# A bidirectional state-space scan: joining the two directions' exponents by a predicated copy instead of mask products

## The chip, the cores and the metric

One core of one Trainium2 chip. The time is device microseconds of one launch; lower is better. All data are fp32, or fp32r, a rounded form in which a product shows as one record instead of two.

## What is computed

Two blocks on 256 tokens of width 1024: the first joins a bidirectional state-space branch (SSD) and windowed attention and is followed by a feed-forward layer, the second has neighbourhood attention, a short convolution and another feed-forward layer. The change is in the state-space branch alone. Cut to what matters:

```python
def segsum_exp(a):
    cs = jnp.cumsum(a, axis=-1)
    diff = cs[..., :, None] - cs[..., None, :]
    mask = jnp.tril(jnp.ones((L, L), dtype=bool))
    return jnp.exp(jnp.where(mask, diff, -jnp.inf))

def ssd_scan(x, dt, a, b, c):          # 8 groups of 4 heads of 64, state 128, chunks of 128
    a_cs = jnp.cumsum(a_dt, axis=-1)
    xdt = x * dt[..., None]
    decay = segsum_exp(a_dt)
    cb = jnp.einsum('bclgn,bcsgn->bcgls', c, b)
    y_diag = jnp.einsum('bcgls,bcgrls,bcsgrp->bclgrp', cb, decay, xdt)
    ...
    y_off = jnp.einsum('bclgn,bcgrpn,bcgrl->bclgrp', c, prev, jnp.exp(a_cs))
    return (y_diag + y_off).reshape(Bsz, S, G, R, P)

y_fwd = ssd_scan(xs, dt[:, :, 0], a[0], bs, cs)
y_bwd = fl(ssd_scan(fl(xs), fl(dt[:, :, 1]), a[1], fl(bs), fl(cs)))
y = y_fwd + y_bwd + xs * d_skip
```

The forward direction fills the triangle s <= l of the decay matrix, the backward one the triangle s >= l. They share only the diagonal, where both exponents of the decay are 0.

## The kernel before, in words

Each engine has its own hand-written program. The weights come as 147 pieces of 128x2048, one per *slot*. For a slot ScalarE makes the rounded high part (`split_hi`, L1068), VectorE the rest (`split_lo`, L1452), both two slots ahead, and TensorE multiplies (`stream`, L606). In a slot of the z and gate projections that is twelve 128x512 products, then what `slot_middle` (L897) puts between, then twelve more. Semaphores order everything: `claim` (L374) makes TensorE wait until the last reader of a PSUM bank is done, `fill_of` and `drain_of` count fills and reads, `ready` and `emptied` wait for them.

The scan runs beside slots 27 to 36, one group g per slot, g = slot - 28. In the order of TensorE, for group g and chunks c of 128 tokens:

- at the end of slot g + 27: `ssd_cb(g)` (L881, bank 7), two fp32 products of 128x128, and `ssd_decay(g, 0)` (L856, banks 5 and 6);
- in the middle of slot g + 28: `ssd_decay(g, 1)`, again into banks 5 and 6, then `ssd_states(g-1)` (bank 7), `ssd_diagonal(g-1)` (L835, bank 4) and `ssd_across(g-1)` (bank 7).

`ssd_decay` makes, for each direction d, four heads' exponents in one product of `cum_s` and `cum_l`. The tables already hold the cumulative sums and the logarithm of dt. Onto this it adds a second product, of the identity `unit` and the mask tile `far`, which holds -1e30 outside the triangle, so that the exponential is 0 there:

```python
pe.matmul(ps[:, 5 + d, :], cum_s[g % 2][:, 2 * c + d, :], cum_l[c][:, d, :, :],
          start=True, stop=False)
pe.matmul(ps[:, 5 + d, :], unit[:, :], far[:, d].unsqueeze(1).to_broadcast([P, PER_GROUP, P]),
          start=False, stop=True).then_inc(*fill_of(key))
```

ScalarE's slot (from L1218) copies `cb` out of bank 7, does `decay_exps(g, 0)` (L1149: one exponential per direction, into `decay` and `decay_back`), then `split_hi(s + 2)`, later the squares of group g - 2, `decay_exps(g, 1)`, the state copy, and after the slots in which a z chunk closes (28 and 30) a Silu of z. VectorE's slot starts with `ssd_weigh(g, 0)` (L1702: add the two directions, multiply by cb), then `split_lo(s + 2)`, `ssd_weigh(g, 1)` and `ssd_gate(g - 1)` (L1713: skip term, y_off from bank 7, y from bank 4, z), and in two of these slots a gate bias. GpSimd makes the state inputs and the rows of the cumulative sums that a group needs, `decay_rows` (L2074). ScalarE's Exp and Silu lie in different function tables, so a table load stands where they alternate.

## Time and profile before

| | |
|---|---|
| median of 3 runs | 943.63 us (942.15 to 943.77) |
| the profiled execution | 942.23 us, of which the span of the instructions is 940.4 us |
| busy in the span | TensorE 932.4 us, VectorE 662.4, ScalarE 507.6, GpSimd 60.8 |
| the scan | about 203 to 298 us |

A busy TensorE row counts a product from its start to its end, and these overlap: what a product costs is the distance from its start to the next start. In a timeline row, "x4" means that four instructions in a row are merged, and the brackets at its end give how long the engine stood idle before it and what released it.

### The profile page before, as it was taken

What the parts mean: (1) busy time and instruction counts of PE and PEld (TensorE: products, weight loads), DVE (VectorE), ACT (ScalarE), POOL (GpSimd) and SP (SyncE); (2) the same over time, 40 slices, a digit from 0 to 9 for tenths busy, and PEclk for the clock granted to TensorE, in tenths of its full rate; (3) what the DMA queues carried; (4) which work ended last, traced back from release to release, by engine and by line L of the source; (5) the groups of instructions that cost most, each with busy time, mean ns of one, the idle gap of its engine ahead of it and who ended that gap; (6) DMA issues with size and microseconds to landing.
All of it is one profiled execution on the core that took longest, in us unless ns stands there. A gap on an engine that the chain in (4) does not pass through costs nothing.

```text
span 940.4 us, 13246 instructions
## 1 busy us (share of the span) xinstructions
PE 932.4 (99%) x5362; PEld 807.9 (86%) x5362; DVE 662.4 (70%) x946; ACT 507.6 (54%) x664; POOL 60.8 (6%) x68
## 2 busy tenths in 40 slices
PE   9999999999999999999999999999999999999998
PEld 8988899988888888888888888899888898888887
DVE  6779789998878764778776446767665758776433
ACT  6457876676555733456554335755653455554331
POOL 1000000023321000000003310000000000000000
PEclk9999999999999999999999999999999999999999
DMA  8943233554224475435447955353355435546551
GB/s 306 341 168 124 93 133 135 180 167 169 91 90 157 140 307 197 169 131 221 179 180 236 256 196 206 136 205 128 123 217 179 179 135 217 187 179 224 178 179 45
DMA packets 25278, 166.51 MB, mean 177 GB/s; under 512 B 2987, under 2 KB 3115, under 8 KB 6657
## 3 DMA queue, kind: packets, MB, share of 16 engines
q1 hardware_dynamic: 22464, 156.12, 46.1%
q0 software_dynamic: 2752, 9.54, 3.5%
q8 instruction: 43, 0.70, 0.3%
q14 instruction: 19, 0.15, 0.0%
HBM read 164.57 MB, written 1.08 MB: 176 GB/s over the span
## 4 chain that ended last, share of the span: by engine, by line
PE 86%; DVE 11%; ACT 2%; issue 1%; ACTq 0%; DVEq 0%
PE ps L393 54%; PE ps L582 11%; PE ps L587 6%; DVE conv_acc L1688 5%; DVE w_lo L1455 3%; PE ps L843 1%; PE ps L772 1%; PE ps L787 1%; PE ps L424 1%; PE ps L426 1%; PE ps L433 1%; PE ps L512 1%; PE ps L630 1%; PE ps L893 1%; PE ps L852 1%
## 5 line engine op out<-in xcount | busy, mean ns | idle before, releaser
L1455 DVE TENSOR_TENSOR w_lo<-raw,w_hi 128x2048 fp32r<-128x2048 f32 x145 | 331.3, 2291 | 181.0 <-ACT w_hi L1075 180.8
L1075 ACT ACTIVATE w_hi<-raw 128x2048 fp32r<-128x2048 f32 x145 | 275.5, 1906 | 179.1 <-PE ps L393 160.2
L393 PE MATMUL ps<-w_hi,ht 128*128 128x512 f32 (+1 forms) x576 | 181.4, 388 | 0.0
L393 PE MATMUL ps<-ht,w_hi 128*128 128x256 f32 (+1 forms) x816 | 150.6, 286 | 0.0
L393 PEld LDWEIGHTS ps<-ht,w_hi 128*128 128x128 f32 (+1 forms) x816 | 126.2, 190 | 4.1 <-issue 4.0
L393 PEld LDWEIGHTS ps<-w_hi,ht 128*128 128x128 f32 x576 | 107.3, 188 | 22.4 <-issue 1.1
L393 PE MATMUL ps<-ht,w_lo 128*128 128x256 f32 (+1 forms) x408 | 115.3, 282 | 0.0
L393 PE MATMUL ps<-w_lo,ht 128*128 128x512 f32 (+1 forms) x288 | 110.5, 384 | 0.0
L582 PE MATMUL ps<-ht,w_hi 128*128 128x512 f32 x448 | 109.5, 391 | 0.0
L393 PE MATMUL ps<-w_hi,ff_hi 128*128 128x512 f32 x256 | 99.7, 389 | 0.0
L393 PE MATMUL ps<-w_lo,ff_hi 128*128 128x512 f32 x256 | 99.6, 389 | 0.0
L393 PE MATMUL ps<-w_hi,ff_lo 128*128 128x512 f32 x256 | 99.6, 389 | 0.0
L582 PEld LDWEIGHTS ps<-ht,w_hi 128*128 128x128 f32 x448 | 81.5, 189 | 15.2
L393 PEld LDWEIGHTS ps<-ht,w_lo 128*128 128x128 f32 (+1 forms) x408 | 77.6, 190 | 0.0
L393 PEld LDWEIGHTS ps<-w_lo,ht 128*128 128x128 f32 x288 | 54.2, 188 | 10.4
L587 PEld LDWEIGHTS ps<-ht,w_lo 128*128 128x128 f32 x448 | 59.3, 191 | 3.3
L587 PE MATMUL ps<-ht,w_lo 128*128 128x256 f32 x448 | 60.3, 282 | 0.0
L393 PEld LDWEIGHTS ps<-w_hi,ff_hi 128*128 128x128 f32 x256 | 48.1, 188 | 10.0
L393 PEld LDWEIGHTS ps<-w_hi,ff_lo 128*128 128x128 f32 x256 | 48.0, 188 | 10.0
L393 PEld LDWEIGHTS ps<-w_lo,ff_hi 128*128 128x128 f32 x256 | 48.1, 188 | 9.8
L1688 DVE SCALAR_TENSOR_TENSOR conv_acc<-conv_in,params,conv_acc 128x256 f32<-128x256 f32 x128 | 52.1, 477 | 0.0
L1190 ACT ACTIVATE ff_sum<-ps 128x512 f32<-128x512 f32 x32 | 18.8, 595 | 35.4 <-PE ps L587 34.4
(301 smaller groups left out, 1217.4 us busy)
## 6 DMA issues: line engine op xcount, KB each, us to landing
raw<-in_w_stream SPq DMA_DIRECT2D x145, 1024.0 KB, 4.8
bias<-rel_scratch POOLq DMA_DIRECT2D x1, 3072.0 KB, 21.2
bias<-in_rpb POOLq DMA_DIRECT2D x16, 128.0 KB, 7.9
x_first<-in_x_in SPq DMA_DIRECT2D x2, 512.0 KB, 4.1
raw<-in_w_stream SPq DMA_DIRECT2D x2, 512.0 KB, 6.4
gates<-in_gate_bias POOLq DMA_DIRECT2D x4, 256.0 KB, 6.0
gates<-in_gate_bias POOLq DMA_DIRECT2D x2, 512.0 KB, 7.2
x<-in_x_in POOLq DMA_DIRECT2D x1, 1024.0 KB, 5.3
```

The lines of the kernel that those rows point to most:

```text
L393: ins = pe.matmul(o, still, moving, start=first and n == 0, stop=last and n == 2, skip_group_check=True)
L424: pe.matmul(ps[:, i, 0:TOK], hi[:, c], ht_hi[:, k, :], start=opens and kt == 0, stop=False, skip_group_check=True)
L426: pe.matmul(ps[:, i, 0:TOK], lo[:, c], ht_hi[:, k, :], start=False, stop=False, skip_group_check=True)
L433: ins = pe.matmul(ps[:, i, TOK:2 * TOK], hi[:, kt * 512 + i * P:kt * 512 + i * P + P], ht_lo[:, 4 * part + kt, :], start=False, stop=close ...
L512: pe.matmul(ps[:, bank0 + r, :], ht_hi[:, 4 * part + kt, tokens], w[:, kt * 512:kt * 512 + 512], start=part == 0 and kt == 0 and m == 0, s ...
L582: pe.matmul(ps[:, 4 * (chunk % 2) + i, :], hi[:, cols(kt, i)], ht[:, :, 4 * part + kt, :], start=opens and kt == 0, stop=False, skip_group ...
L587: ins = pe.matmul(ps[:, 4 * (chunk % 2) + i, 0:TOK], lo[:, cols(kt, i)], ht_hi[:, 4 * part + kt, :], start=False, stop=closes and kt == 3, ...
L630: pe.matmul(ps[:, 2 * n + r, :], a_hi[:, kt, r * P:r * P + P], w[:, cols], start=kt == 0 and m == 0, stop=False, skip_group_check=True)
L1075: act.activation(split_home(s)[0][:, 0:width(s)], raw[s % RAW_RING][:, 0:width(s)], ACT.Copy).then_inc(hi_ready, 1)
L1190: act.activation(ff_sum[half][:, :, :], ps[:, b:b + 2, TOK:2 * TOK], ACT.Copy).then_inc(lows_out, 1)
L1455: dve.tensor_tensor(lo[:, 0:width(s)], raw[s % RAW_RING][:, 0:width(s)], hi[:, 0:width(s)].bitcast(F32), ALU.subtract).then_inc(lo_ready, 1)
L1688: ins = dve.scalar_tensor_tensor(acc_of(c)[:, i, :], conv_in[k][:, i, tap:tap + TOK], conv_w[:, tap, f:f + 1], acc_of(c)[:, i, :], ALU.mul ...
```

## The change

The mask products go. Both directions' exponents still land in banks 5 and 6. VectorE then copies, where s > l, bank 6 over bank 5 (`copy_predicated`, in PSUM, with the 0/1 triangle `tri[:, 2]` as predicate), and ScalarE takes one exponential of bank 5 per chunk. The addition of the two directions goes. On the diagonal only the forward value is left, so the backward direction's own term is computed apart: `twins` = B times C, summed over the state by 16 products with a column of ones, times dt, added to the skip factor once (`own_terms`). The rows of the cumulative sums of groups 1 to 7 move from GpSimd to ScalarE, behind its exponentials. ScalarE's first exponential of a slot moves behind its weight split, its second behind the state copy. VectorE's second weighing moves into the gate of the group before, behind the skip term.

```diff
+        twins = at("twins", [P, GROUPS, TOK], 146496)
+        own_skip = at("own_skip", [P, RT, HEADS], 158784)
...
                 pe.wait_ge(cum_s_ready, g + 1)
-                if g == 0 and c == 0:
-                    pe.wait_ge(far_ready, 1)
                 for d in range(2):
                     key = ("decay", g, c, d)
                     claim(key, 5 + d)
                     pe.matmul(ps[:, 5 + d, :], cum_s[g % 2][:, 2 * c + d, :], cum_l[c][:, d, :, :],
-                              start=True, stop=False)
-                    pe.matmul(ps[:, 5 + d, :], unit[:, :], far[:, d].unsqueeze(1).to_broadcast([P, PER_GROUP, P]),
-                              start=False, stop=True).then_inc(*fill_of(key))
+                              start=True, stop=True).then_inc(*fill_of(key))
+
+            def twin_sums():
+
+                claim("twins", 4)
+                pe.wait_ge(twins_ready, 1)
+                for c in range(RT):
+                    for g in range(GROUPS):
+                        at0 = c * GROUPS + g
+                        ins = pe.matmul(ps[:, 4, at0:at0 + 1], twins[:, g, c * P:c * P + P], tri[:, 0, P - 1:P],
+                                        start=True, stop=True)
+                ins.then_inc(*fill_of("twins"))
...
                     ssd_decay(s - 28, 1)
+                    if s == 28:
+                        twin_sums()
...
             def decay_exps(g, c):
-                for d, dest in enumerate((decay[g % 2][c], decay_back[c])):
-                    key = ("decay", g, c, d)
-                    ready(act, key)
-                    if d == 0 and g >= 2:
-                        ready(act, ("y", g - 2))
-                    if d == 1 and g:
-                        act.wait_ge(decay_scaled, 2 * g - 1 + c)
-                    act.activation(dest[:, :, :], ps[:, 5 + d, :].rearrange("p (h l) -> p h l", h=PER_GROUP),
-                                   ACT.Exp).then_inc(*drain_of(key))
+                key = ("decay", g, c, 0)
+                emptied(act, ("decay", g, c, 1))
+                if g == 1 and c == 0:
+                    ready(act, "twins")
+                if g >= 2:
+                    ready(act, ("y", g - 2))
+                act.activation(decay[g % 2][c][:, :, :], ps[:, 5, :].rearrange("p (h l) -> p h l", h=PER_GROUP),
+                               ACT.Exp).then_inc(*drain_of(key))
...
                                    ACT.Copy).then_inc(*drain_of(key))
-                    decay_exps(g, 0)
                 late = s in (S_MI - 1, S_MI2 - 1)
                 if s + AHEAD < SLOTS and s != S_Q2 - 1 and not late:
                     split_hi(s + AHEAD)
                 if s == S_Q2 - 2:
                     split_hi(S_Q2 + 1)
+                if 0 <= s - 28 < GROUPS:
+                    decay_exps(s - 28, 0)
...
-                if 0 <= s - 28 < GROUPS:
-                    decay_exps(s - 28, 1)
                 if 0 <= s - 29 < GROUPS:
                     key = ("state", s - 29)
                     ready(act, key)
                     act.activation(state[:, :, :], ps[:, 7, :].rearrange("p (a b) -> p a b", a=2),
                                    ACT.Copy).then_inc(*drain_of(key))
+                if 0 <= s - 28 < GROUPS:
+                    decay_exps(s - 28, 1)
+                if 0 <= s - 28 < GROUPS - 1:
+                    g = s - 27
+                    if g == 1:
+                        act.wait_ge(cum_s_ready, 1)
+                    else:
+                        ready(act, ("decay", g - 2, 1, 1))
+                    act.activation(cum_s[g % 2][:, :, :], cum[:, :, :], ACT.Identity, scale=quad[:, 10 + g:11 + g],
+                                   bias=quad[:, 18 + g:19 + g]).then_inc(cum_s_ready, 1)
...
+            def ssd_choose(g, c):
+
+                ready(dve, ("decay", g, c, 0)), ready(dve, ("decay", g, c, 1))
+                both = [ps[:, 5 + d, :].rearrange("p (h l) -> p h l", h=PER_GROUP) for d in range(2)]
+                dve.copy_predicated(both[0], tri[:, 2].bitcast(I32).unsqueeze(1).to_broadcast([P, PER_GROUP, P]),
+                                    both[1]).then_inc(*drain_of(("decay", g, c, 1)))
+
             def ssd_weigh(g, c):
 
-                emptied(dve, ("decay", g, c, 0)), emptied(dve, ("decay", g, c, 1))
-                w = decay[g % 2][c]
-                link(dve.tensor_tensor(w[:, :, :], w[:, :, :], decay_back[c][:, :, :], ALU.add))
+                emptied(dve, ("decay", g, c, 0))
...
+            def own_terms():
+
+                ready(dve, "twins")
...
                 for c in range(RT):
                     v = xtok(c, g * GW, GW).rearrange("p (h d) -> p h d", h=PER_GROUP)
-                    ins = dve.tensor_tensor(v, v, per_head(param("d_skip")[:, 4 * g:4 * g + 4], 4), ALU.mult)
+                    ins = dve.tensor_tensor(v, v, per_head(own_skip[:, c, 4 * g:4 * g + 4], 4), ALU.mult)
                 link(ins)
+                if g + 1 < GROUPS:
+                    ssd_weigh(g + 1, 1)
...
                 if 0 <= s - 28 < GROUPS:
-                    ssd_weigh(s - 28, 0)
+                    ssd_choose(s - 28, 0)
...
+                if s == 27:
+                    dve.wait_ge(conv_silu, 8)
+                    dve.tensor_tensor(twins[:, :, :], bc[:, 0:GROUPS, :], bc[:, GROUPS:2 * GROUPS, :],
+                                      ALU.mult).then_inc(twins_ready, 1)
                 if 0 <= s - 28 < GROUPS:
-                    ssd_weigh(s - 28, 1)
+                    ssd_weigh(s - 28, 0)
+                    ssd_choose(s - 28, 1)
+                if s == 28:
+                    ssd_weigh(0, 1)
+                    own_terms()
```

How the instructions now stand, at three places. First ScalarE, in the slots of groups 0 and 1; `w_hi` is the high part of a weight piece. Before:

```order
L1075 ACTIVATE w_hi_54<-raw_51 128x2048
L1227 ACTIVATE cb<-ps 128x256
L1157 ACT_TABLE_LOAD
L1157 ACTIVATE decay_0_107<-ps 128x512
L1157 ACTIVATE decay_back_111<-ps 128x512
L1075 ACTIVATE w_hi_52<-raw_49 128x2048
L1157 ACTIVATE decay_1_108<-ps 128x512
L1157 ACTIVATE decay_back_112<-ps 128x512
L1329 ACT_TABLE_LOAD
L1329 ACTIVATE zg_90<-ps 128x512 x2
L1227 ACTIVATE cb<-ps 128x256
L1157 ACT_TABLE_LOAD
```

With the change:

```order
L1083 ACTIVATE w_hi_54<-raw_51 128x2048
L1234 ACTIVATE cb<-ps 128x256
L1083 ACTIVATE w_hi_52<-raw_49 128x2048
L1164 ACT_TABLE_LOAD
L1164 ACTIVATE decay_0_107<-ps 128x512
L1164 ACTIVATE decay_1_108<-ps 128x512
L1339 ACTIVATE cum_s_124<-cum,params 128x512
L1345 ACT_TABLE_LOAD
L1345 ACTIVATE zg_90<-ps 128x512 x2
L1234 ACTIVATE cb<-ps 128x256
L1083 ACTIVATE w_hi_53<-raw_50 128x2048
L1164 ACT_TABLE_LOAD
```

The first exponential of each slot, with its table load, now stands behind the weight split, and there is one exponential per chunk.

Second VectorE, from the subtraction for slot 28 to the first work of group 1; `w_lo` is the low part of a weight piece. Before:

```order
L1455 TENSOR_TENSOR w_lo_56<-raw_50,w_hi_53 128x2048
L1455 TENSOR_TENSOR w_lo_57<-raw_51,w_hi_54 128x2048
L1706 TENSOR_TENSOR decay_0_107<-decay_0_107,decay_back_111 128x512
L1709 TENSOR_TENSOR decay_0_107<-decay_0_107,cb 128x512
L1455 TENSOR_TENSOR w_lo_55<-raw_49,w_hi_52 128x2048
L1706 TENSOR_TENSOR decay_1_108<-decay_1_108,decay_back_112 128x512
L1709 TENSOR_TENSOR decay_1_108<-decay_1_108,cb 128x512
L1706 TENSOR_TENSOR decay_0_109<-decay_0_109,decay_back_111 128x512
L1709 TENSOR_TENSOR decay_0_109<-decay_0_109,cb 128x512
```

With the change:

```order
L1471 TENSOR_TENSOR w_lo_56<-raw_50,w_hi_53 128x2048
L1471 TENSOR_TENSOR w_lo_57<-raw_51,w_hi_54 128x2048
L1925 TENSOR_TENSOR twins<-bc 128x2048
L1722 COPY_PREDICATED ps<-params,ps 128x512
L1471 TENSOR_TENSOR w_lo_55<-raw_49,w_hi_52 128x2048
L1731 TENSOR_TENSOR decay_0_107<-decay_0_107,cb 128x512
L1722 COPY_PREDICATED ps<-params,ps 128x512
L1731 TENSOR_TENSOR decay_1_108<-decay_1_108,cb 128x512
L1740 TENSOR_TENSOR own_skip<-dt,ps 128x32 x2
L1745 TENSOR_TENSOR own_skip<-own_skip,params 128x64
```

The product of B and C stands ahead of the first predicated copy, and the copies stand where the weighing of the same chunk stood.

Third TensorE, in the middle of the slot of group 0, with the change; before, four products (two of them of `far`) stood between the stream products, and no `twins`:

```order
L392 MATMUL ps<-w_hi_53,ht 128x512 x2
L392 MATMUL ps<-w_lo_56,ht 128x512
L392 MATMUL ps<-w_hi_53,ht 128x512
L862 MATMUL ps<-cum_l_122,cum_s_123 128x512 x2
L872 MATMUL ps<-params,twins 128x1 x16
L392 MATMUL ps<-w_hi_53,ht 128x512
L392 MATMUL ps<-w_lo_56,ht 128x512
```

The 16 one-column products come behind the second chunk's exponents of group 0, once in the program.

## Rows read from the trace of the kernel before

**Rows 1.** The page: busy time by engine, the clock by slice, the chain that ended last.
```profile
PE 932.4 (99%) x5362; PEld 807.9 (86%) x5362; DVE 662.4 (70%) x946; ACT 507.6 (54%) x664; POOL 60.8 (6%) x68
...
PEclk9999999999999999999999999999999999999999
...
PE 86%; DVE 11%; ACT 2%; issue 1%; ACTq 0%; DVEq 0%
```

**Rows 2.** List of waits, TensorE: us in total, times, longest.
```profile
PE ps L915 <- DVE warm L1474: 1.5, 1, 1.5
```

**Rows 3.** Timeline, TensorE, groups 3 and 4: start us, duration us, instruction.
```profile
246.33 0.48 PE L865 MATMUL ps<-cum_l,cum_s 128*128 128x512 f32 x1
...
257.32 0.60 PE L884 MATMUL ps<-bc 128*128 128x128 f32 x4
257.68 0.48 PE L865 MATMUL ps<-cum_l,cum_s 128*128 128x512 f32 x1
```

**Rows 4.** Timeline, TensorE, middle of the slot of group 1.
```profile
215.27 0.39 PE L865 MATMUL ps<-cum_l,cum_s 128*128 128x512 f32 x1
...
216.19 1.02 PE L852 MATMUL ps<-x_state,btok 128*128 128x256 f32 x4
```

**Rows 5.** Timeline, TensorE: products of 32 and of 64 moving columns, and what follows.
```profile
68.03 0.98 PE L831 MATMUL ps<-adt,params 128*128 128x32 f32 x8
68.84 0.63 PE L787 MATMUL ps<-params,logit 128*128 128x128 f32 x4
...
217.05 1.89 PE L843 MATMUL ps<-xtok,decay 128*128 128x64 f32 x16
218.78 1.08 PE L893 MATMUL ps<-state,bc 128*128 128x256 f32 x4
```

**Rows 6.** Timeline, TensorE, slot of group 0.
```profile
203.69 0.48 PE L865 MATMUL ps<-cum_l,cum_s 128*128 128x512 f32 x1
204.01 0.40 PE L867 MATMUL ps<-far,unit 128*128 128x512 f32 x1
...
207.47 0.40 PE L865 MATMUL ps<-cum_l,cum_s 128*128 128x512 f32 x1
```

**Rows 7.** Timeline, ScalarE, slot of group 4.
```profile
257.96 0.39 ACT L1227 ACTIVATE cb<-ps 128x256 f32<-128x256 f32 x1 [5.26 <-PE ps L884]
...
259.40 1.92 ACT L1075 ACTIVATE w_hi<-raw 128x2048 fp32r<-128x2048 f32 x1
261.20 0.41 ACT L1316 ACTIVATE junk<-xtok 128x256 f32<-128x256 f32 x1
```

**Rows 8.** Timeline, ScalarE, slot of group 0.
```profile
204.61 1.28 ACT L1157 ACT_TABLE_LOAD   x1
205.90 0.60 ACT L1157 ACTIVATE decay<-ps 128x512 f32<-128x512 f32 x1
```

**Rows 9.** Timeline, VectorE, slots of groups 0 and 1: weight subtractions and what follows.
```profile
204.36 2.46 DVE L1455 TENSOR_TENSOR w_lo<-raw,w_hi 128x2048 fp32r<-128x2048 f32 x1 [0.73 <-ACT w_hi L1075]
...
217.16 2.29 DVE L1455 TENSOR_TENSOR w_lo<-raw,w_hi 128x2048 fp32r<-128x2048 f32 x1 [0.31 <-ACT w_hi L1075]
219.37 1.10 DVE L1706 TENSOR_TENSOR decay<-decay,decay_back 128x512 f32<-128x512 f32 x1
```

**Rows 10.** Timeline, TensorE: first exponents of groups 1, 2 and 3.
```profile
211.52 0.48 PE L865 MATMUL ps<-cum_l,cum_s 128*128 128x512 f32 x1
...
223.48 0.48 PE L865 MATMUL ps<-cum_l,cum_s 128*128 128x512 f32 x1
...
234.82 0.48 PE L865 MATMUL ps<-cum_l,cum_s 128*128 128x512 f32 x1
```

**Rows 11.** One line's instructions, VectorE: duration ns min/median/max, first and last start.
```profile
L1728 DVE TENSOR_TENSOR xtok<-ps,xtok x8: 681/681/682, 222.9 to 298.5; 128x512 f32<-128x512 f32 x8
```

**Rows 12.** The same for ScalarE, line 1297: 256 elements, two column operands.
```profile
L1297 ACT ACTIVATE conv_acc<-conv_in,params x32: 588/592/597, 61.9 to 189.2; 128x256 f32<-128x256 f32 x32
```

**Rows 13.** Timeline, TensorE, start of the program.
```profile
1.45 5.49 PE L915 MATMUL ps<-warm 128*128 128x512 f32 x12 [1.45 <-DVE warm L1474]
```

More of the change, by code:

```diff
@@ L258, in build @@
                  for i in range(2)]
-        decay_back = [at(f"decay_back{c}", [P, PER_GROUP, P], 150592 + 2048 * c) for c in range(RT)]
+        twins = at("twins", [P, GROUPS, TOK], 146496)
         cb = at("cb", [P, RT, P], 154688)
-        far = at("far", [P, 2, P], 141376, F32R)
         ndt = at("ndt", [P, RT, 2 * HEADS], 158272)
-        unit = at("unit", [P, P], 158784, F32R)
+        own_skip = at("own_skip", [P, RT, HEADS], 158784)
         adt_wide = at("adt_wide", [P, 4, 4, HEADS], 175968)
@@ L331, in build @@
         ndt_ready = sem("ndt_ready")
-        decay_scaled, far_ready, x_state_ready = sem("decay_scaled"), sem("far_ready"), sem("x_state_ready")
+        decay_scaled, twins_ready, x_state_ready = sem("decay_scaled"), sem("twins_ready"), sem("x_state_ready")
         pool_chain = sem("pool_chain")
@@ L1700, in per_head @@
                 return values.unsqueeze(2).to_broadcast([P, count, HD])
+            def ssd_choose(g, c):
[3 more added lines that the diff above has]
+                                    both[1]).then_inc(*drain_of(("decay", g, c, 1)))
             def ssd_weigh(g, c):
-                emptied(dve, ("decay", g, c, 0)), emptied(dve, ("decay", g, c, 1))
-                w = decay[g % 2][c]
-                link(dve.tensor_tensor(w[:, :, :], w[:, :, :], decay_back[c][:, :, :], ALU.add))
+                emptied(dve, ("decay", g, c, 0))
                 if c == 0:
                     emptied(dve, ("cb", g))
+                w = decay[g % 2][c]
                 dve.tensor_tensor(w[:, :, :], w[:, :, :],
@@ L1711, in ssd_weigh @@
                                   ALU.mult).then_inc(decay_scaled, 1)
+            def own_terms():
+                ready(dve, "twins")
+                v = own_skip[:, :, :].rearrange("p c (g h) -> p c g h", g=GROUPS)
+                for c in range(RT):
+                    ins = dve.tensor_tensor(v[:, c], dt[:, c, HEADS:2 * HEADS].rearrange("p (g h) -> p g h", g=GROUPS),
+                                            ps[:, 4, c * GROUPS:c * GROUPS + GROUPS].unsqueeze(2)
+                                            .to_broadcast([P, GROUPS, PER_GROUP]), ALU.mult)
+                ins.then_inc(*drain_of("twins"))
+                emptied(dve, "twins")
+                link(dve.tensor_tensor(own_skip[:, :, :], own_skip[:, :, :],
+                                       param("d_skip").unsqueeze(1).to_broadcast([P, RT, HEADS]), ALU.add))
             def ssd_gate(g):
@@ L2072, in state_inputs @@
                                        ALU.mult).then_inc(x_state_ready, 1)
-            def decay_rows(g):
-                if g >= 2:
-                    ready(pool, ("decay", g - 2, 1, 0))
-                pool.tensor_scalar(cum_s[g % 2][:, :, :], cum[:, :, :], quad[:, 10 + g:11 + g],
-                                   quad[:, 18 + g:19 + g], ALU.mult, ALU.add).then_inc(cum_s_ready, 1)
             pool.wait_ge(params_landed, 16)
-            pool.tensor_copy(unit[:, :], ident)
             pool.wait_ge(tables_ready, 1)
-            decay_rows(0)
-            pool.wait_ge(conv_silu, 7)
-            pool.tensor_scalar(far[:, :, :], tri[:, 2:4], NEG, None, ALU.mult).then_inc(far_ready, 1)
+            pool.tensor_scalar(cum_s[0][:, :, :], cum[:, :, :], quad[:, 10:11], quad[:, 18:19],
+                               ALU.mult, ALU.add).then_inc(cum_s_ready, 1)
             pool.wait_ge(conv_silu, 8)
@@ L2098, in _ @@
                                        ).then_inc(gate_bias_landed, 16)
-                if g + 1 < GROUPS:
-                    decay_rows(g + 1)
             pool.wait_ge(cum_s_ready, GROUPS)
-            ready(pool, ("decay", GROUPS - 1, 1, 0))
+            ready(pool, ("decay", GROUPS - 1, 1, 1))
             for cols, done in ((slice(512, 1024), gate_bias_second), (slice(1024, 2 * D), gate_bias_rest)):
```

## The prediction

> **What bounds the kernel now.** I read the page first. TensorE is busy for 932.4 of 940.4 us, its granted clock is full in every slice, and the chain that ended last runs through it for 86% [rows 1]. The list of who waited for whom, for TensorE alone, has seven lines, 4.7 us together; the largest, at the start of the program, is 1.5 us [rows 2], and one of 0.4 lies in the scan. So the time is the sum of what TensorE issues, plus its waits. Work that the change takes from VectorE, ScalarE or GpSimd is worth nothing by itself; a wait that it makes for TensorE is paid in full.
>
> The timeline of the scan gives TensorE's rhythm. One slot holds twelve stream products, the second chunk's exponents, states, diagonal and across products, twelve more, then the next group's cb and first exponents. The first chunk's exponents of groups 3 and 4 start at 246.33 and 257.68 us, 11.35 apart [rows 3]. Behind the first of four exponent products the next work comes after 216.19 - 215.27 = 0.92 us, so they follow each other every 0.23 us [rows 4].
>
> **What is removed.** The mask products are 32 instructions of 128x512. At 0.23 us of start to start [rows 4] that is 32 x 0.23 = **-7.4 us**, all of it on TensorE's path.
>
> **What TensorE gets.** 16 twin products of a full stationary tile and one moving column. fp32 products show as two records each (the eight diagonal products are 16 records), so 32 records. No row has one column. With 64 columns, 16 records take 218.78 - 217.05 = 1.73 us, 0.108 each; with 32 columns eight take 68.84 - 68.03 = 0.81, 0.101 each [rows 5]. Halving the columns hardly helped, so the weight load seems to set the pace; I take 0.101, **+3.2 us**. The ends are 0.108 (3.5 us) and, if a single column could be half as dear, 1.6 us.
>
> **Where TensorE will wait.** The exponents keep using banks 5 and 6. The second chunk's product into bank 5 waits until ScalarE has read the first chunk's bank 5. Before, ScalarE did both exponentials ahead of its 1.9 us weight split. Now it does the split first, and the exponential also waits for VectorE's predicated copy. In which slots does that show?
>
> *Steady slots.* Counted from the first cb product of the slot: TensorE comes back for bank 5 after 0.36 (cb, 257.32 to 257.68 [rows 3]) and what lies between the first and the second chunk's exponents: in group 0 that was 207.47 - 203.69 = 3.78 [rows 6], now less two mask products, 3.32. Together 3.68 us. ScalarE starts the cb copy 0.64 after the cb product (257.96 - 257.32 [rows 3, 7]), may go on 0.39 later, the split holds it for 261.20 - 259.40 = 1.80 [rows 7] and the exponential lasts 0.60 [rows 8], together 3.43 us. There is 0.25 us to spare: no wait, but nearly one. VectorE's copy is ready for it: both products have landed by about 1.3, and the copy takes 0.7.
>
> *Group 1 and group 3.* The silu of z before them changes ScalarE's tables, and the load of 1.28 us for Exp [rows 8] now stands behind the split, just ahead of the exponential. 3.43 + 1.29 = 4.72 against 3.68: with the delay of a signal TensorE waits **1.1 us, twice, +2.2 us**. Before, the same load was hidden, since no split stood ahead of the exponential.
>
> *Group 0.* The load is there too, but something later decides. VectorE issues the product B times C (128x2048) right behind the split of slot 29, and the first predicated copy behind it. That split starts at 204.36 and lasts 2.46 [rows 9], so the twin product starts near 206.8. Like the subtraction at 217.16, whose successor starts 2.21 us later [rows 9], it holds the engine for 2.2 us, to 209.0. Copy 0.69, exponential 0.60: bank 5 is free at 210.3. TensorE, less two mask products, is there at 207.47 - 0.46 = 207.0 [rows 6]. **+3.3 us** in one piece.
>
> *Restart.* After each of these three waits the weights were not loaded ahead; the first exponent product behind cb starts the next one after 0.32 us where 0.23 is usual [rows 6]. +0.1 each, **+0.3 us**.
>
> **What else goes.** In the slot of group 1, TensorE waited for VectorE's y_off before it could use bank 7: from the exponents of group 1 to those of group 2 it is 223.48 - 211.52 = 11.96 us, where the next is 234.82 - 223.48 = 11.34 [rows 10]. Following the new order, y_off is done over a microsecond before the cb product: **-0.6 us**. A 0.2 us late state copy in group 2's slot (group 3's exponents come 246.33 - 234.82 = 11.51 after the last [rows 3, 10]) goes with the order of the table load, **-0.2 us**.
>
> **Costed at nothing.** The predicated copy stands on VectorE for the addition of the two directions. No row shows such an instruction. The nearest, a 128x512 read of PSUM, takes 0.68 [rows 11], the removed addition up to 1.10 [rows 9]. I take 0.69. Its ends are 0.6 and two passes, 1.4 us; the upper end adds 0.7 to group 0's wait and makes VectorE late in the slot with the gate bias, some 0.5 more. The cumulative rows on ScalarE: two column operands and 512 elements, between 0.6 for an exponential and perhaps 0.8 from the 0.59 that 256 elements with two columns take [rows 8, 12]. They are done some 2 us before TensorE's next exponents; if ScalarE ran that much later they would become the wait. GpSimd loses its part of the rows; this only shortens VectorE instructions that ran beside it, which are off the path. Skip multiplication, own_skip, the mask tile: small, on VectorE, and covered.
>
> On the table load: the exponential begins 1.29 us after the load starts, 204.61 to 205.90 [rows 8], and I count 1.29. The Trainium skill, page "ScalarE: Activation LUTs", section "What ACT_TABLE_LOAD costs", counts about 2.66 us for a switch, the load and a drain. By that page each of the waits of groups 1 and 3 would be some 1.4 us longer and the sum 2.7 us higher; the row decides against it.
>
> **Sum.** -7.4 + 3.2 + 3.3 + 2.2 + 0.3 - 0.6 - 0.2 = +0.8 us. The profiled execution took 942.23 us, so 943.0 by it. The median of the three runs, 943.63, stands 1.4 above it, within their spread of 942.15 to 943.77. Set on the median the forecast is **944.4 us**. About 0.2%, 1.9 us, is what a measurement of this kernel tells from no change; the forecast lies inside it.
>
> **Rivals.**
> *A, slower: the long wait costs clock.* TensorE stands still for over 3 us in group 0, longer than any wait in the trace [rows 2]. At the start of the program, after idling, twelve 128x512 products take 5.49 us, some 0.45 each, nearly twice the 0.23 of the scan [rows 4, 13], though the page's clock row is at its top there too [rows 1]; I read that pace as the 1.2 GHz level against 2.4. If the clock falls, a like stretch costs 12 x 0.22 = 2.6 us more: 947.0. It decides from the wait on, if the wait is long enough. For it: the size of the wait. Against: no row shows a fall after work. The Trainium skill, page "TensorE: Matmul & The Clock Gate", section "What's actually happening", says that an idle array is put back to half its clock until it has been kept busy again.
>
> *B, slower: the predicated copy is dear.* At 1.4 us or with the 0.25 us margin of the steady slots used up, group 0 waits 0.7 more and some of the five steady slots wait 0.1 to 0.5: +1.5 to +2.5, about 946.4.
>
> *C, faster: the waits don't come.* If ScalarE or VectorE is free earlier than I think, so that group 0 waits under 1 us and the others not at all, the sum is -7.4 + 3.2 + 1.0 - 0.8 = -4.0: 939.6. If only the twins are cheap, -0.8: 942.8. For it: everything before fitted without waits. Against: the order of the instructions and their durations.
>
> *D: the mask products are not the cost they seem,* because they ran under another limit. Then nothing is gained: +7 us. Against: in the timeline they take their 0.23 us with TensorE at no wait. 2%.
>
> **Chances.** Forecast 0.64, A 0.10, B 0.11, C 0.13, D 0.02. Around the forecast itself, 942.5 to 946, about 0.12 of its 0.64 ends more than 1.9 us above 943.63. Slower: 0.12 + 0.10 + 0.08 of B + 0.02 = 0.32. Faster by 1.9 us: most of C and a trace of the rest, 0.14. Within: 0.54. The range goes from cheap twins less the scatter of the runs shown (942.8 - 1.2), 941.6, to A with some scatter, 947.2.
>
> **What would show it.** The exponent products 32 in number; twin records near 0.10 us apart. In the list of waits TensorE waits for ScalarE's exponential three times: over 3 us at about 207 us, then 1.1 at about 221 and 243 us. The slots of groups 4 to 7 are 10.4 us apart. Wrong would be: no such waits; waits in all eight slots (B); 128x512 products 0.44 us apart behind the long wait (A); a predicated copy far from 0.7.

## The result and the profile after

| | before | changed |
|---|---|---|
| median | 942.89 us (942.1 to 943.77, 4 runs) | 949.06 us (946.9 to 949.73, 4 runs) |
| profiled execution | 942.23 us, span 940.4 | 948.48 us, span 946.7 |
| ratio | | 1.0062, 95% interval 1.0049 to 1.0075 |

The change makes the kernel slower by 0.6%, about 6 us, where 944.4 us with an upper end of 947.2 was forecast. The executions of the kernel before lie at two levels, near 942.2 and, with a mean granted clock of 0.998 instead of 1.00 in the experiments' runs of it, near 943.7; the change is outside both.

Two lines from the page of the changed kernel, to compare with [rows 1]:

```profile
PE 933.3 (99%) x5362; PEld 809.2 (85%) x5362; DVE 658.4 (70%) x950; ACT 504.9 (53%) x655; POOL 42.8 (5%) x59
...
PEclk9999999998999999999999999999999999999999
```

TensorE is still busy for 99% of the span, but in the tenth slice the clock row shows 8 where all the others show 9. The list of waits for TensorE (us in total, times, longest):

```profile
PE ps L862 <- ACT decay L1164: 5.4, 3, 3.2
```

5.4 us in three waits for ScalarE's exponential, with a longest of 3.2, is what the forecast had, 3.3 + 1.1 + 1.1. TensorE's timeline of the slots of groups 0 and 1 (compare [rows 6]):

```profile
203.66 0.72 PE L862 MATMUL ps<-cum_l,cum_s 128*128 128x512 f32 x2
...
210.33 1.01 PE L862 MATMUL ps<-cum_l,cum_s 128*128 128x512 f32 x2 [3.19 <-ACT decay L1164]
211.14 6.82 PE L872 MATMUL ps<-params,twins 128*128 128x1 f32 x32
217.82 0.77 PE L392 MATMUL ps<-w_hi,ht 128*128 128x512 f32 x1
...
226.97 0.70 PE L862 MATMUL ps<-cum_l,cum_s 128*128 128x512 f32 x2 [1.10 <-ACT decay L1164]
```

The same timeline at the exponents of group 3, 4 and 5:

```profile
249.12 0.70 PE L862 MATMUL ps<-cum_l,cum_s 128*128 128x512 f32 x2 [1.09 <-ACT decay L1164]
...
256.30 0.72 PE L862 MATMUL ps<-cum_l,cum_s 128*128 128x512 f32 x2
...
266.73 0.71 PE L862 MATMUL ps<-cum_l,cum_s 128*128 128x512 f32 x2
```

The first exponents of groups 4 and 5 are 266.73 - 256.30 = 10.43 us apart, where [rows 3] has 11.35: the four mask products of a slot are gone, and that saves 0.92. But the 32 records of the twin products, between 211.14 and 217.82, take 6.68 us, 0.209 each, twice what was forecast. The reason stands in the table of stretches (us, then busy time and, in brackets, instructions of TensorE, its weight loads, VectorE, ScalarE and GpSimd, then TensorE's granted clock, the DMA share and GB/s):

```profile
204.00:208.00 4.00, 3.14 (x14) 2.24 (x12) 3.72 (x2) 3.61 (x4) 1.70 (x4) 1.00 0.83 287
208.00:212.00 4.00, 1.67 (x7) 1.50 (x8) 4.00 (x4) 0.60 (x1) 0.00 (x0) 0.82 0.91 240
212.00:216.00 4.00, 4.00 (x20) 4.00 (x20) 1.65 (x3) 2.98 (x4) 0.00 (x0) 0.50 0.98 369
216.00:220.00 4.00, 4.00 (x15) 3.61 (x15) 0.51 (x3) 0.20 (x1) 0.00 (x0) 0.50 0.05 23
220.00:224.00 4.00, 4.00 (x19) 3.28 (x19) 0.70 (x1) 1.76 (x3) 0.00 (x0) 0.90 0.00 0
```

From about 210.5 to 220.8 us the granted clock is 0.50, the 1.2 GHz level. Before the fall TensorE had stood still from 207.1 to 210.3, and the fall comes with the exponent products, before the first one-column product at 211.14; while the clock was low, TensorE issued two exponent products, the one-column products and nearly 3 us of stream products, and then it rose. In half-microsecond stretches the clock missing from 1.00 adds up to 5.1 us; this sum is called the loss by the clock below. 3.2 of it are in the one-column products (6.68 us against 3.49 at the full clock in e3).

VectorE's and ScalarE's timelines show how the wait comes about (compare [rows 8, 9]). VectorE in the slot of group 0:

```profile
204.28 2.47 DVE L1471 TENSOR_TENSOR w_lo<-raw,w_hi 128x2048 fp32r<-128x2048 f32 x1 [0.73 <-ACT w_hi L1083]
206.67 2.28 DVE L1925 TENSOR_TENSOR twins<-bc 128x2048 f32<-128x2048 f32 x1
208.87 0.68 DVE L1722 COPY_PREDICATED ps<-params,ps 128x512 f32<-128x512 int32 x1
```

ScalarE in the same stretch, and its load and exponential in the slot of group 1:

```profile
204.41 1.91 ACT L1083 ACTIVATE w_hi<-raw 128x2048 fp32r<-128x2048 f32 x1
206.34 1.28 ACT L1164 ACT_TABLE_LOAD   x1
209.59 0.60 ACT L1164 ACTIVATE decay<-ps 128x512 f32<-128x512 f32 x1 [1.97 <-DVE ps L1722]
...
224.93 1.28 ACT L1164 ACT_TABLE_LOAD   x1
226.22 0.60 ACT L1164 ACTIVATE decay<-ps 128x512 f32<-128x512 f32 x1
```

ScalarE's table is loaded at 207.6, then it waits for the predicated copy. The copy waits for the product of B and C in front of it. The predicated copies by their source line (duration ns min/median/max, then when they run):

```profile
L1722 DVE COPY_PREDICATED ps<-params,ps x16: 684/693/697, 208.9 to 292.9; 128x512 f32<-128x512 int32 x16
```

The cumulative rows that ScalarE now makes, in the same view:

```profile
L1339 ACT ACTIVATE cum_s<-cum,params x7: 803/804/813, 213.5 to 283.7; 128x512 fp32r<-128x512 f32 x7
```

### The profile page after: what moved, and what is told of

It reads as the page before. It is cut to its first block, busy times and chain, and to the rows that moved or that the text cites. A ratio compares the mean times of both kernels' runs of the same rounds, so it can differ in the third digit from the quotient of the medians.

```text
span 946.7 us, 13221 instructions
## 1 busy us (share of the span) xinstructions
PE 933.3 (99%) x5362; PEld 809.2 (85%) x5362; DVE 658.4 (70%) x950; ACT 504.9 (53%) x655; POOL 42.8 (5%) x59
## 3 DMA queue, kind: packets, MB, share of 16 engines
HBM read 164.57 MB, written 1.08 MB: 175 GB/s over the span
## 4 chain that ended last, share of the span: by engine, by line
PE 85%; DVE 11%; ACT 2%; issue 1%; DMA 0%; SPq 0%; ACTq 0%; DVEq 0%
PE ps L392 54%; PE ps L581 11%; PE ps L586 6%; DVE conv_acc L1704 5%; DVE w_lo L1471 3%; PE ps L842 1%; PE ps L771 1%; PE ps L786 1%; PE ps L423 1%; PE ps L425 1%; PE ps L432 1%; PE ps L511 1%; PE ps L899 1%; PE ps L629 1%; PE ps L862 1%
```

## The experiments

All are compared with runs of the kernel before on the same chip, whose medians lie between 942.2 and 942.3 us. Theory 1 was that the long wait costs the clock; theory 2 that the one-column products do.

**e1, the wait filled with work.** 13 products of 128x512, whose results nobody reads, ahead of the second chunk's exponents. They go into the twin products' bank, and the claim of that bank moves with them.

```diff
+                    if s == 28:
+                        claim("twins", 4)
+                        for _ in range(13):
+                            pe.matmul(ps[:, 4, :], cum_s[0][:, 0, :], cum_l[0][:, 0, :, :], start=True, stop=True)
                     ssd_decay(s - 28, 1)
```

> The changed kernel with 13 extra 128x512 products (their result is thrown away) on TensorE just ahead of the second chunk's exponents of group 0, where it stands still for 3.2 us. Theory 1, the long wait costs the clock: the products fill the wait (13 x 0.23 = 3.0 us), the clock stays full, the 32 one-column records take 3.2 us instead of 6.7, and the time falls from 949.1 by about 5.1 to 944.0 us although work was added. Theory 2, the one-column products themselves cost the clock and the wait is innocent: the fall comes just the same, the time stays within 1 us of 949.1.

Measured: 946.67 us (945.18 to 946.94), ratio 1.0041, 1.0029 to 1.0054. TensorE's timeline, with the filling at 206.88:

```profile
206.88 3.16 PE L914 MATMUL ps<-cum_l,cum_s 128*128 128x512 f32 x13
210.25 0.70 PE L862 MATMUL ps<-cum_l,cum_s 128*128 128x512 f32 x2 [0.21 <-ACT decay L1167]
210.79 3.63 PE L871 MATMUL ps<-params,twins 128*128 128x1 f32 x32
```

And its stretches, columns as above:

```profile
208.00:212.00 4.00, 3.79 (x23) 3.02 (x22) 4.00 (x4) 0.60 (x1) 0.00 (x0) 1.00 0.93 254
212.00:216.00 4.00, 4.00 (x27) 3.71 (x27) 2.08 (x6) 3.06 (x4) 0.00 (x0) 0.85 0.88 352
216.00:220.00 4.00, 4.00 (x16) 3.21 (x16) 0.08 (x1) 1.21 (x4) 0.00 (x0) 0.72 0.04 18
```

The clock is full through the filled wait and at the start of the twin products. Then, near 214.8, half a microsecond behind the last twin product, it falls all the same and is back near 218.2; the loss is 1.7 us instead of 5.1. Three microseconds of useless products made the kernel faster: by 2.4 us in the medians, and by 948.48 - 945.18 = 3.3 in the profiled executions, where 3.4 less is lost by the clock. (The profiled one is e1's fastest; three of the five lie at 946.7 to 946.9 with a mean granted clock of 0.996, as does the fastest of the changed kernel.) The expected 944.0 us of theory 1 was not reached. So the idle time was a cause. But it was not the only one: neither theory holds alone.

**e2, the wait without the one-column products.** One product with 16 moving columns takes the place of the sixteen; the backward direction's own terms are left out by it, and only the time is of use.

```diff
-                for c in range(RT):
-                    for g in range(GROUPS):
-                        at0 = c * GROUPS + g
-                        ins = pe.matmul(ps[:, 4, at0:at0 + 1], twins[:, g, c * P:c * P + P], tri[:, 0, P - 1:P],
-                                        start=True, stop=True)
+                ins = pe.matmul(ps[:, 4, 0:2 * GROUPS], twins[:, 0, 0:P], tri[:, 0, 0:2 * GROUPS],
+                                start=True, stop=True)
```

> The changed kernel with 1 of the 16 twin products; the backward direction's own terms are left out by that. The wait of 3.2 us in group 0 stays. Theory 1: the clock still falls as TensorE resumes at 210.3, but comes back some 3 us later, since full products follow at once; the loss by the clock is about 1.5 us instead of 5.1, so 949.1 - 3.0 - 3.6 = 942.5 us. Theory 2: no fall at all, 949.1 - 3.0 - 5.1 = 941.0 us and a granted clock of 1.00 throughout.

Measured: 943.12 us (942.4 to 944.03), ratio 1.0007, 0.9998 to 1.0016. The stretches:

```profile
208.00:212.00 4.00, 1.67 (x5) 1.50 (x6) 4.00 (x4) 0.60 (x1) 0.00 (x0) 0.66 0.86 220
212.00:216.00 4.00, 4.00 (x10) 3.06 (x10) 2.07 (x6) 2.98 (x4) 0.00 (x0) 0.50 0.96 377
216.00:220.00 4.00, 4.00 (x21) 3.30 (x19) 1.28 (x2) 3.47 (x5) 0.00 (x0) 0.99 0.10 41
```

The fall comes, with one short product in place of sixteen, and it comes near 209.3, a microsecond before TensorE issues anything again: the wait suffices. The clock is low for some 6.8 us in this profile. That is a loss of 3.4 us, of which some 0.5 falls into the wait and costs nothing; the rest, 2.9, is about twice the 1.5 expected. TensorE resumed at 210.3 and the clock rose near 216.1, 5.7 us later: mostly full products do not bring it back as fast as I thought. In three of the eleven executions (942.4 to 942.5 us) the mean granted clock is 0.998 or 0.999 instead of 0.996, so the loss is smaller there.

**e3, a shorter wait.** The product of B and C moves behind the first predicated copy, the twin products to the end of the slot.

```diff
             for s in range(SLOTS):
                 if 0 <= s - 28 < GROUPS:
                     ssd_choose(s - 28, 0)
+                if s == 28:
+                    dve.wait_ge(conv_silu, 8)
+                    dve.tensor_tensor(twins[:, :, :], bc[:, 0:GROUPS, :], bc[:, GROUPS:2 * GROUPS, :],
+                                      ALU.mult).then_inc(twins_ready, 1)
...
+                if s == 28:
+                    twin_sums()
                 if 0 <= s - 27 < GROUPS:
```

> The changed kernel with VectorE's product of B and C behind the first predicated copy, and the 16 twin products at the end of the slot of group 0. The wait in group 0 then lasts until the table load is through: about 1.3 us instead of 3.2. Theory 1: the clock stays full, the time is 949.1 - 1.9 - 5.1 = 942.1 us. Theory 2: the clock falls at the twin products, wherever they stand: about 947 us. The waits of groups 1 and 3 stay at 1.1 us in both.

Measured: 942.51 us (942.2 to 945.26), ratio 1.0004, 0.9995 to 1.0012. TensorE's timeline:

```profile
208.36 0.70 PE L862 MATMUL ps<-cum_l,cum_s 128*128 128x512 f32 x2 [1.24 <-ACT decay L1164]
...
211.66 3.63 PE L872 MATMUL ps<-params,twins 128*128 128x1 f32 x32
215.15 0.72 PE L890 MATMUL ps<-bc 128*128 128x128 f32 x4
```

The stretches of the same kernel:

```profile
208.00:212.00 4.00, 3.64 (x18) 3.08 (x19) 4.00 (x3) 0.22 (x1) 0.00 (x0) 1.00 0.99 225
212.00:216.00 4.00, 4.00 (x35) 4.00 (x35) 2.14 (x6) 3.00 (x4) 0.00 (x0) 0.96 0.98 383
216.00:220.00 4.00, 4.00 (x12) 3.08 (x12) 1.92 (x2) 3.98 (x5) 0.00 (x0) 0.61 0.06 25
```

The wait is 1.24 us and the clock stands through it. Behind the twin products, which now take 215.15 - 211.66 = 3.49 us at the full clock, it falls near 215.6 as in e1, for 1.7 us of loss. The time agrees with theory 1's number, but the clock row doesn't: the 942.1 us had no second fall in it, and the waits of groups 0 and 3 are all that is left, since in the slot of group 1 TensorE itself is late by the low clock. Theory 2's 947 us is out as well: theory 1's number is right in part by luck.

**e4, the exponential ahead of the split in groups 1 and 3.**

```diff
+                    if g in (1, 3):
+                        decay_exps(g, 0)
...
-                if 0 <= s - 28 < GROUPS:
+                if 0 <= s - 28 < GROUPS and s - 28 not in (1, 3):
                     decay_exps(s - 28, 0)
```

> The changed kernel with the first exponential ahead of the weight split in the slots of groups 1 and 3, those with a table load. Both theories: TensorE's waits of 1.1 us there go and no other comes, 949.1 - 2.2 = 946.9 us; the fall of the clock in group 0 stays. If the later weight split makes VectorE late instead, TensorE waits for VectorE's low part or copy in those slots and nothing is gained.

Measured: 948.33 us (948.2 to 948.54), ratio 1.0064, 1.0051 to 1.0076. The two waits are gone from TensorE's list:

```profile
PE ps L862 <- ACT decay L1164: 3.2, 1, 3.2
```

But the median is only 0.7 us below the changed kernel's, where 2.2 were expected, and the ratios don't differ. Two things eat the gain. In this profile the clock is low from 209.8 to 223.5 us, a loss of 6.8 where the changed kernel's has 5.1; the fall again comes within the long wait. And TensorE has two new waits for y_off, of 0.3 us each, where none was expected: from the exponents of group 1 to those of group 2 it is 10.95 us and from those of group 3 to those of group 4 10.99, against 11.72 and 11.74 in the changed kernel and 10.43 in a slot without a wait. The executions of the changed kernel themselves differ in this: their mean granted clock is 0.992 in the two of 949.7 us, 0.995 in that of 948.5 and 0.996 in that of 946.9. So e4 can't show the full 2.2 us beside a loss that moves by 1.7. Set beside the two executions of like clock, 949.6 and 949.7 us, e4's 948.2 to 948.5 are 1.1 to 1.5 us shorter, as are these two slots together (1.5).

**e5, e6, e7: no waits, and the twin products in three forms.** All three have the product of B and C and the first predicated copy ahead of the subtraction for slot 29, and the first exponential ahead of the split in groups 0, 1 and 3. Common to the three:

```diff
+                if s == 27:
+                    dve.wait_ge(conv_silu, 8)
+                    dve.tensor_tensor(twins[:, :, :], bc[:, 0:GROUPS, :], bc[:, GROUPS:2 * GROUPS, :],
+                                      ALU.mult).then_inc(twins_ready, 1)
+                    ssd_choose(0, 0)
...
+                    if g in (0, 1, 3):
+                        decay_exps(g, 0)
```

Theory 3 is that the run of one-column products makes the clock fall by itself, theory 4 that a fall needs a wait of TensorE ahead of it. e5 has the 16 one-column products unbroken at the end of the slot, as e3. e6 gives each of them 32 columns of ones:

```diff
-                        ins = pe.matmul(ps[:, 4, at0:at0 + 1], twins[:, g, c * P:c * P + P], tri[:, 0, P - 1:P],
+                        ins = pe.matmul(ps[:, 4, 32 * at0:32 * at0 + 32], twins[:, g, c * P:c * P + P],
+                                        tri[:, 0, P - 1:P].to_broadcast([P, 32]),
```

e7 puts four of them behind every three stream products:

```diff
+                            if s == 28 and half == 1:
+                                twin_sums(kt)
```

> The changed kernel with all three waits of TensorE removed by order alone: VectorE does the product of B and C and the first predicated copy ahead of the weight subtraction for slot 29, ScalarE the first exponential ahead of the weight split in the slots of groups 0, 1 and 3; the 16 twin products come unbroken at the end of the slot of group 0. Theory 3, an unbroken run of one-column products costs the clock by itself: no wait for ScalarE is left, but the clock falls behind the twin products for about 3 us (1.6 us lost); from the run before with one wait of 1.2 and one of 1.1 left (942.5) this takes 2.3 and two restarts: 940.0 us. Theory 4, a fall needs a wait of TensorE ahead of it: no fall, 938.3 us.

> The kernel of the run e5 with 32 moving columns, all ones, in each of the 16 twin products instead of one. The records keep their distance of about 0.10 us (32 columns took 0.101 in the kernel before). Theory 3: the clock stays full if it is the idle columns that count, 938.4 us; if it is the run of short products as such, as in e5. Theory 4: as e5.

> The kernel of the run e5 with the 16 twin products in four parts of four, each behind three stream products of 128x512 in the second half of the slot of group 0. Theory 3: the clock stays full, 1.6 us less than e5, 938.4 us, which is 942.2 - 7.4 + 3.2 - 0.8 with some tenths for the change between the forms. Theory 4: as e5.

Measured: e5 942.29 us (940.32 to 943.31), ratio 0.9998, 0.9990 to 1.0007; e6 940.67 us (940.08 to 942.12), ratio 0.9982, 0.9973 to 0.9990; e7 940.76 us (940.68 to 942.19), ratio 0.9985, 0.9976 to 0.9994. The twin products of e5 and its stretches:

```profile
210.49 4.74 PE L872 MATMUL ps<-params,twins 128*128 128x1 f32 x32
...
208.00:212.00 4.00, 4.00 (x27) 3.53 (x25) 4.00 (x4) 0.84 (x1) 0.00 (x0) 1.00 0.86 156
212.00:216.00 4.00, 4.00 (x24) 4.00 (x24) 1.61 (x5) 3.53 (x5) 0.00 (x0) 0.60 0.96 387
216.00:220.00 4.00, 4.00 (x12) 3.15 (x11) 0.70 (x1) 3.77 (x5) 0.00 (x0) 0.55 0.28 117
```

The stretches of e7:

```profile
212.00:216.00 4.00, 4.00 (x27) 3.62 (x27) 2.27 (x6) 3.56 (x6) 0.00 (x0) 1.00 1.00 281
216.00:220.00 4.00, 3.38 (x17) 2.56 (x16) 0.00 (x0) 3.97 (x5) 0.00 (x0) 1.00 0.46 190
```

In e5 no wait of TensorE stands before the fall; the clock falls near 212.8, amid the one-column products that began at 210.49, and returns near 219.5, a loss of 3.4 us. Theory 4 is out for this fall: an unbroken run of them is enough. In e7 the same 16 products, spread, leave the clock at 1.00. So they do in e6's profile with 32 columns. Over all executions the mean granted clock is 0.999 or 1.000 in 9 of 11 of e7 and in 6 of 11 of e6, and 0.996 to 0.998 in the others; in e5 it is 0.995 to 0.998 in all. The two of e7 at 0.998 lie 1.4 us above the rest, as do 12 of the 58 executions of the kernel before, which has no twin products; nothing shows that they are to blame there. In e6, three executions at 0.998 (940.08 to 940.49 us) are even shorter than those at 1.00 (940.59 to 941.0). They are not of the long kind; most likely the clock falls in the scan there and hides a wait, as in e5, but their profiles were not kept. Spreading is thus the surer way.

e5's profile has a second low stretch far from the scan, for another 1.7 us of loss:

```profile
405.57 0.83 PE L721 MATMUL ps<-params,x 128*128 128x128 f32 x4 [1.08 <-DVE x L1569]
406.78 0.35 PE L423 MATMUL ps<-ht,w_hi 128*128 128x256 f32 x1 [0.37 <-ACT ht L1106]
...
408.00:412.00 4.00, 4.00 (x25) 4.00 (x25) 3.29 (x4) 1.42 (x1) 0.00 (x0) 0.66 0.00 0
```

The clock is low from 407.3 to 410.7, behind two waits of 1.08 and 0.37 us that the kernel before has too, with the same lengths and, in its profile, no fall. That fits the kernel before's own executions at 943.7 us; but no profile of one was kept, so where their clock falls is not shown. It also gives e5's time: the expected 940.0 us counted 1.6 for the clock, the profile has 3.4 + 1.7, and 940.0 + 3.5 = 943.5 stands against 943.17 measured.

What e6 and e7 save by the clock they partly give back in new waits, and so they miss the expected 938.4 us by 2.3. From e7's list for TensorE:

```profile
PE ps L893 <- DVE y_off L1764: 1.5, 2, 1.2
...
PE ps L864 <- ACT decay L1165: 0.6, 1, 0.6
```

With the exponential first, the split of group 1 ends later, the low part later still, and VectorE's y_off late enough for TensorE to wait 1.2 us before the cb product of group 2. In e5 the low clock hid these.

**e8, the price of a mask product.** The kernel before with each mask product issued twice.

```diff
                     pe.matmul(ps[:, 5 + d, :], unit[:, :], far[:, d].unsqueeze(1).to_broadcast([P, PER_GROUP, P]),
-                              start=False, stop=True).then_inc(*fill_of(key))
+                              start=False, stop=False)
+                    pe.matmul(ps[:, 5 + d, :], unit[:, :], far[:, d].unsqueeze(1).to_broadcast([P, PER_GROUP, P]),
+                              start=False, stop=True).then_inc(*fill_of(key))
```

> The kernel before with each mask product issued twice (the exponents outside the triangle are -2e30 instead of -1e30, which changes nothing). If a mask product costs 0.23 us on the path, as the forecast has it: 942.2 + 32 x 0.23 = 949.6 us. If the scan has another limit, the added products cost less than that.

Measured: 948.63 us (948.53 to 948.68), ratio 1.0066, 1.0054 to 1.0078, so +6.3 us. A slot grows from 11.34 [rows 10] to 236.88 - 224.65 = 12.23 us, 0.22 per added product:

```profile
224.65 0.48 PE L865 MATMUL ps<-cum_l,cum_s 128*128 128x512 f32 x1
...
236.88 0.48 PE L865 MATMUL ps<-cum_l,cum_s 128*128 128x512 f32 x1
```

That is 7.1 us for 32; TensorE's wait for y_off in the scan is no longer in the list, which takes 0.4 to 0.6 back. The run's expected 949.6 us counted 0.23 for each and nothing back, and was 1.0 too high. The mask products cost nearly what was forecast, 7.1 against 7.4 us, all of it on the path.

**e9, the best order found.** e7 with y_off ahead of the second weighing and the Silu of slot 28 joined to that of slot 30, so that one pair of table loads goes; group 1 then needs no exponential ahead of its split.

```diff
                 ready(dve, ("off", g))
...
                 ins.then_inc(*drain_of(("off", g)))
+                if g + 1 < GROUPS:
+                    ssd_weigh(g + 1, 1)
...
-                if name == "z" and closes:
-                    for r in range(RT):
+                if name == "z" and closes and chunk != 2:
+                    for chunk, r in [(k, r) for k in ((2, 3) if chunk == 3 else (chunk,)) for r in range(RT)]:
```

> The kernel of the run e7 with three changes of order against its remaining waits: the y_off products of VectorE go ahead of the second weighing, the Silu of the z chunk of slot 28 is done together with that of slot 30 (one pair of table loads less), and so group 1 needs no exponential ahead of its split. If TensorE's waits for y_off (1.5 us) and for ScalarE's exponential (0.6 us) are all that is left between the sum and the time: 940.75 - 2.1 - 0.3 = 938.3 us, with no wait over 0.1 us in the scan. If another wait comes up behind them, it stays near 940.

Measured: 938.29 us (938.13 to 939.68), ratio 0.9957, 0.9944 to 0.9969. It beats both kernels, and lands on the expected number. TensorE's list of waits has nothing from the scan left; its first line is that of the program's start:

```profile
PE ps L924 <- DVE warm L1493: 1.4, 1, 1.4
```

And the clock holds, as the stretches show:

```profile
212.00:216.00 4.00, 4.00 (x28) 3.62 (x28) 2.34 (x6) 2.56 (x4) 0.00 (x0) 1.00 0.95 274
216.00:220.00 4.00, 4.00 (x24) 3.49 (x23) 3.04 (x4) 2.02 (x3) 0.67 (x1) 1.00 0.48 201
```

**e10, wide twin products behind the long wait.** The changed kernel with e6's 32 columns and the longer wait left as it is.

> The changed kernel with 32 moving columns of ones in each twin product, the wait of 3.2 us left as it is. If the wait makes the clock fall and the one-column products only keep it low: it falls as before near 210.4 but returns earlier, in one profile perhaps 6 us later instead of 10 or 13, and the time is 949.1 - 1.6 = 947.5 us or less. If the number of columns has no part in it: 949.1.

Measured: 948.59 us (948.47 to 948.72), ratio 1.0064, 1.0050 to 1.0078. The clock is low from about 210.7 to 221.0, again 5.1 us of loss, and the 32 records last as long as with one column:

```profile
210.30 0.81 PE L862 MATMUL ps<-cum_l,cum_s 128*128 128x512 f32 x2 [3.21 <-ACT decay L1164]
210.90 6.87 PE L872 MATMUL ps<-params,twins 128*128 128x32 f32 x32
```

Theory 1's half of the expectation, 947.5 us or less, is a miss: with more columns the clock did not fall in e6's profile, but here, once fallen, it came back no sooner. The time and the loss are the same with 1 and with 32 columns, so what the columns do behind a long wait doesn't show.

## Why the prediction was wrong, point by point

- *Mask products removed, -7.4 us.* Right: 0.92 a slot in the steady slots, 7.1 by doubling them in e8.
- *Twin products, +3.2 us.* A little low at the full clock: 3.49 us in e3, 0.109 per record, the upper one of the two rows that it was read from (0.108 and 0.101). A single column isn't cheaper than 32, which take 3.49 us in e6 too. At the low clock it was 6.68.
- *Three waits, +5.5 us.* Right in place, cause and size: 3.19, 1.10 and 1.09, by the timeline, against 3.3, 1.1 and 1.1. So were the predicated copy (0.69 us) and the cumulative rows on ScalarE (0.80 us, waited for by nobody).
- *Restarts, +0.3 us.* Low: the slots of groups 1 and 3 last 11.72 and 11.74 us beside 10.43, 1.3 more for waits of 1.1, so 0.2 each.
- *The table load at 1.29 us, not 2.66.* Right: the exponential of group 1 starts at 226.22, the load at 224.93. The Trainium skill's figure of 2.66 us with a drain (page "ScalarE: Activation LUTs", section "What ACT_TABLE_LOAD costs") fits no row here.
- *Waits that go, -0.8 us.* Right: neither y_off nor the state copy holds TensorE in the changed kernel.
- *Numbering.* By [rows 10] the exponents at 246.33 and 257.68 us of [rows 3] are those of groups 4 and 5, not 3 and 4; no term changes by it.
- *The clock.* This is the step that failed. It stood outside the sum, as rival A with a chance of 0.10 and a price of 12 products, 2.6 us. It came in all four executions by their granted clock (0.992 to 0.996), and costs 5.1 us in the profiled one. Two things were wrong. The chance was low: a wait longer than any in the trace had been computed, the trace before could not say what it does to the clock, and I counted "no row shows a fall after work" against it, although no row showed such a wait either. And the price was taken from twelve full products at the program's start, a stretch of 5.5 us. Here the clock stayed low for 10.2 us, and the one-column products that followed the wait lasted 6.68 us instead of 3.49 and were over before it rose; e2 shows 5.7 us at half pace even with one short product and full ones behind it.
- *The median, 943.63 us.* Two of the three executions shown were the long kind, near 943.7. The 1.4 us that they stand above the profiled one were taken for scatter; executions of that length in the experiments (12 of 58) all show a mean granted clock of 0.998. Set on 942.2 the forecast would have been 943.0, farther from the result.

With the clock the sum closes: -7.4 + 3.5 + 5.4 + 0.6 - 0.8 + 5.1 = +6.4 us. The profiled executions differ by 948.48 - 942.23 = 6.25.

A second way of losing the clock was not foreseen at all: e1, e3 and e5 show that the unbroken run of one-column products makes the clock fall even where TensorE never stood still (e5). In the changed kernel the fall belongs to the wait: it comes 0.6 us before the first of them, and within the wait itself in e2 and e4. What the run adds to the length of the low stretch can't be told from one profile each, 10.2 us with it and 6.8 without.

The Trainium skill, "TensorE: Matmul & The Clock Gate", section "What's actually happening", says that the throttled state is the default and that activity releases it. e2 agrees for the long wait, with 0.50 from 209.3 us on, and every low stretch in the scan ended while TensorE was busy; e5's fall at 212.8 with no idle time ahead of it, and e3's 7 us behind its wait, are nothing that an idle array explains.

What stays open: what decides the length of a low stretch (losses of 5.1 and 6.8 us in profiles of kernels alike in that place); what in a run of one-column products makes the clock fall, since with 32 columns it was full in some executions and most likely fell in others; and where it drops in the executions at 0.998 of the kernel before, of e7 and of e9 (one of five, 939.68 us).

## What to carry to other kernels

When TensorE is busy all the time, a wait that a change makes for it costs its own length and can then cost the clock: with 3.2 us it did in every profile, with 1.24 us (e3) it did not, and behind waits of 1.08 and 0.37 us it did in one profile of several (e5). Price both, and what runs right behind the wait at half pace. Work taken off TensorE is worth having only if the waits that its new order makes are removed too: the same change with the copy, the exponentials and the Silu put where their results are due, and with the twin products spread, was 3.9 us faster than the kernel before instead of 6.2 slower. Spread runs of tiny products among full ones.

## What the runs showed of the hardware that was not expected

Sixteen products of 128x128 by one column, issued without a break, take 0.109 us per record, as long as with 32 columns (e6) or 64 (0.108), and the granted clock falls to 0.50 behind them (e1, e3) or amid them, with no idle time ahead (e5); the same sixteen in fours between 128x512 products leave it at 1.00 in the scan in the profiles of e7 and e9. The clock can fall behind waits as short as 1.08 and 0.37 us (e5, at 407.3) that in other profiles of the same place leave it full. Thirteen useless products in an idle gap of 3.2 us made the kernel 2.4 us faster by the medians (e1). A 128x512 predicated copy within PSUM takes 0.69 us on VectorE, as a plain read of PSUM does (0.68).
